# A two-layer diffusion-transformer block with attention, convolution and expert lookup: shorter lead of queries and routing, and a re-spaced plan of hosted work

## What is computed

```python
y, y_x = token_mixer(modulate(x, sh1, sc1), modulate(ctx, xsh1, xsc1), w_in, ...)   # dense GQA, short conv, banded attention, gates, w_out
x = layer_norm(alpha * x + g1 * y, ln1_g, ln1_b)
f = peer(modulate(x, sh2, sc2), w_pq, sub_keys, u_tab, v_tab)
x = layer_norm(alpha * x + g2 * f, ln2_g, ln2_b)
# (the same for ctx in layer 0)

def peer(...):                                  # one block of 128 tokens
    q = (xb @ w_pq).reshape(128, 8, 2, 128)     # 8 heads, two halves
    s = einsum('thpd,hpnd->thpn', q, sub_keys)  # 128 keys each half
    s1, i1 = top_k(s[:, :, 0], 16); s2, i2 = top_k(s[:, :, 1], 16)
    cand = s1[..., :, None] + s2[..., None, :]  # 256 pairs
    top, pos = top_k(cand, 16); expert = i1 * 128 + i2 at pos
    g = softmax(top)
    u = u_tab[expert]; v = v_tab[expert]        # 16384 experts a layer
    return einsum('thk,thkd->td', gelu(einsum('td,thkd->thk', xb, u)) * g, v)
```

## Time and profile before

| what | us |
|---|---|
| median of 3 runs | 4705.17 |
| lowest, highest | 4694.17, 4723.45 |
| the profiled execution | 4714.67 |
| its span (first to last instruction) | 4712.6 |
| TensorE, VectorE, ScalarE, GpSimd busy | 3173.5, 2879.9, 830.9, 2790.2 |
| moved by DMA | 1718.66 MB, mean 365 GB/s |

### The profile page before, as it was taken

One profiled execution on the slowest core, in us unless ns is written; L12 is line 12 of the kernel. 1 busy time (PEld: TensorE's weight loads), 2 busy tenths in 40 slices (PEclk: granted clock), 3 DMA queues, 4 the chain that ended last, 5 costly groups with the idle time before them and its releaser, 6 DMA issues.

```text
span 4712.6 us, 47030 instructions
## 1 busy us (share of the span) xinstructions
PE 3173.5 (67%) x16180; PEld 1609.4 (34%) x16180; DVE 2879.9 (61%) x7309; ACT 830.9 (18%) x1946; POOL 2790.2 (59%) x2623
## 2 busy tenths in 40 slices
PE   7977787977778887655653786767797845433333
PEld 4443354444444344322320432544444422200000
DVE  4865566466676587456766652476646766665652
ACT  1321213122122131101110110210312211010000
POOL 1125565457666676666677664046655677777776
PEclk8988897998888988767765898888898976666656
DMA  8879999999999999999999998489999999999998
GB/s 314 321 274 402 371 407 350 369 365 383 401 395 379 409 363 400 407 402 392 392 345 354 410 398 339 145 308 405 335 377 375 380 388 389 366 366 353 371 361 327
DMA packets 494093, 1718.66 MB, mean 365 GB/s; under 512 B 54177, under 2 KB 74913, under 8 KB 493473
## 3 DMA queue, kind: packets, MB, share of 16 engines
q0 software_dynamic: 375552, 1367.51, 75.6%
q1 hardware_dynamic: 100640, 335.04, 18.5%
q10 hardware_dynamic: 17664, 13.11, 0.8%
HBM read 1700.25 MB, written 15.20 MB: 364 GB/s over the span
## 4 chain that ended last, share of the span: by engine, by line
PE 32%; POOL 23%; DMA 15%; issue 12%; DVE 10%; another core or an unknown queue 5%; ACT 3%; SPq 0%; ACTq 0%; POOLq 0%; DVEq 0%
PE ps L967 30%; POOL vr L940 12%; POOL ur L927 10%; DMA vr<-in_v_tab,idxT 10%; DVE ur L2023 2%; PE ps L970 2%; DMA ur<-in_u_tab,idx 2%; DMA wring<-in_w_gb 1%; ACT arena L1429 1%; DVE mx L1891 1%; DMA wring<-in_w_mod 1%; POOL ur L940 0%; DMA wring<-in_w_qkv 0%; DMA wring<-in_w_out 0%
## 5 line engine op out<-in xcount | busy, mean ns | idle before, releaser
L2023 DVE CUSTOM_DVE_ANT_0 ur<-ur,hn 128x1024 f32<-128x1024 f32 x1280 | 1561.7, 1220 | 812.1 <-DMA ur<-in_u_tab,idx 732.6
L940 POOL DMA_INDIRECT vr<-in_v_tab,idxT x1256 | 1381.0, 1100 | 930.9 <-PE ps L967 499.0
L927 POOL DMA_INDIRECT ur<-in_u_tab,idx x1280 | 1357.3, 1060 | 787.1 <-issue 364.5
L967 PE MATMUL ps<-vr,spread 128*32 128x512 f32 x5024 | 896.7, 827 | 927.1 <-DMA vr<-in_v_tab,idxT 842.1
L967 PE MATMUL ps<-wring,arena 128*128 128x512 f32 x2240 | 1033.5, 612 | 76.8 <-ACT arena L1429 23.8
L967 PEld LDWEIGHTS ps<-vr,spread 128*32 128x32 f32 x5024 | 182.5, 135 | 1436.8 <-issue 1426.1
L967 PEld LDWEIGHTS ps<-wring,arena 128*128 128x128 f32 x2240 | 421.3, 195 | 628.3 <-issue 554.9
L967 PE MATMUL ps<-hT,wring 128*128 128x128 f32 (+1 forms) x2048 | 332.7, 321 | 30.5 <-DMA wring<-in_w_pq 22.8
L967 PEld LDWEIGHTS ps<-hT,wring 128*128 128x128 f32 x2048 | 300.7, 207 | 104.4 <-issue 62.6
L967 PE MATMUL ps<-arena,wring 128*128 128x258 f32 (+1 forms) x960 | 225.2, 394 | 7.3 <-issue 5.8
L970 PE MATMUL ps<-ident,arena 128*128 128x128 f32 x888 | 154.2, 311 | 110.7 <-issue 39.5
(11 more groups left out here) (204 smaller groups left out, 2941.9 us busy)
## 6 DMA issues: line engine op xcount, KB each, us to landing
wring<-in_w_gb SPq DMA_DIRECT2D x224, 512.0 KB
wring<-in_w_pq SPq DMA_DIRECT2D x128, 512.0 KB
wring<-in_w_qkv SPq DMA_DIRECT2D x68, 512.0 KB
wring<-in_w_out SPq DMA_DIRECT2D x64, 512.0 KB
wring<-in_w_conv SPq DMA_DIRECT2D x60, 512.0 KB
wring<-in_w_mod SPq DMA_DIRECT2D x48, 512.0 KB
vr<-in_w_modt POOLq DMA_DIRECT2D x48, 512.0 KB
ur<-in_u_tab,idx POOLq DMA_INDIRECT x1280
```

The lines of the kernel that those rows point to most:

```text
L927: nc.gpsimd.indirect_dma_start(u, None, u_rows, bass.IndirectOffsetOnAxis(ap=idx[:, at:at + 1], axis=0)).then_inc(landed, 16)
L940: nc.gpsimd.indirect_dma_start(v, None, v_rows, bass.IndirectOffsetOnAxis(ap=idxT[:, pair % 3, i:i + 1], axis=0)).then_inc(landed, 16)
L967: return nc.tensor.matmul(o, lhsT, rhs, start=first, stop=last, skip_group_check=True)
L2023: v.tensor_tensor_reduce(u, u, hn[:], 1.0, 0.0, ALU.mult, ALU.add, dots[:, j % 2, k:k + 1]).then_inc(s["dots_done"], 1)
```

## The change

`LEAD` is 2 and `LAG` is 1. `lead(n)` makes the queries and scores of two heads and the routing of one. A head's routing runs in the first eight slots of the head before it, two steps in each; ScalarE's exponential moves from slot 11 to slot 5. TensorE's transposition of the picks moves from slot 1 to slot 10, and `turn_picks` on VectorE from slot 3 to slot 10, of the same head. The `turn` steps move to slots 93 to 98, and the blocks of hosted work are re-spaced around them; the attention of tile 3 stays in tile 1, its `merge_last` moves to slots 0 to 16 of tile 2. A second modulation frees the banks, and `merge_far` has a wait for the copy of hn, because of the new order.

```diff
-LEAD = 3
-LAG = 2
+LEAD = 2
+LAG = 1
...
-        for jj, st in ((0, 0), (0, 1), (0, 2), (1, 0), (0, 3), (1, 1), (1, 2), (0, 4), (2, 0), (1, 3), (2, 1), (2, 2), (1, 4)):
+        for jj, st in ((0, 0), (0, 1), (0, 2), (1, 0), (0, 3), (1, 1), (1, 2), (0, 4)):
...
             put(near_part(1, team=1) + merge_first(1) + ending(1), 0, 62)
-            put(keys_job(1), 62, 74)
-            put([[("turn", 1)], [("row", 0)], [("row", 1)], [("row", 2)]], 74, 78)
-            put(keys_job(2) + queries_job(1) + conv_job(1), 78, 126)
+            put(keys_job(1) + keys_job(2), 62, 82)
+            put(queries_job(1), 82, 96)
+            put([[("turn", 1)], [("row", 0)], [("row", 1)], [("row", 2)]], 96, 100)
+            put(conv_job(1), 100, 126)
         elif n == 1:
-            put(near_part(2, 3, team=2) + merge_first(2) + ending(2), 0, 84)
-            put([[("turn", 2)]], 84, 85)
-            put(ending(3), 86, 126)
+            put(near_part(2, 3, team=2) + merge_first(2) + ending(2), 0, 96)
+            put([[("turn", 2)]], 97, 98)
+            put(attention([(3, q) for q in range(4, 8)]), 99, 126)
         elif n == 2:
-            put(queries_job(2)[0:1], 0, 1)
-            put(queries_job(2)[1:] + conv_job(2), 3, 34)
-            put([loads_of(4, 5, team=3)], 34, 35)
-            put(near_part(4, 5)[1:], 36, 74)
-            put([[("turn", 3)], [("row", 3)]], 74, 76)
-            put(merge_first(3), 78, 126)
+            put(merge_last(3), 0, 16)
+            put(queries_job(2)[0:1], 16, 17)
+            put(queries_job(2)[1:] + conv_job(2), 19, 46)
+            put([loads_of(4, 5, team=3)], 46, 47)
+            put(near_part(4, 5)[1:], 48, 78)
+            put(merge_first(3)[0:16], 78, 94)
+            put([[("turn", 3)], [("row", 3)]], 95, 97)
+            put(merge_first(3)[16:], 98, 126)
         elif n == 3:
             put(ending(4, 5), 0, 66)
             put(keys_job(3), 66, 82)
-            put([[("turn", 4)], [("turn", 5)]], 82, 85)
-            put(modulations(BY_PRODUCT[4:]), 84, 126)
+            put(modulations(BY_PRODUCT[4:6]), 83, 92)
+            put([[("turn", 4)], [("turn", 5)]], 93, 96)
+            put(modulations(BY_PRODUCT[6:]), 98, 126)
...
         elif n == 6:
             put(ending(7), 0, 30)
             put(queries_job(4)[0:1], 30, 31)
-            put(queries_job(4)[1:] + conv_job(4), 34, 70)
-            put([loads_of(8, 9, team=5)], 70, 71)
-            put([[("turn", 7)], [("row", 4)], [("row", 5)], [("row", 6)]], 74, 78)
-            put(near_part(8, 9)[1:] + merge_first(5)[0:16], 78, 126)
+            put(queries_job(4)[1:] + conv_job(4), 33, 62)
+            put([loads_of(8, 9, team=5)], 62, 63)
+            put(near_part(8, 9)[1:], 64, 94)
+            put([[("turn", 7)], [("row", 4)], [("row", 5)], [("row", 6)]], 95, 99)
+            put(merge_first(5)[0:16], 100, 126)
         elif n == 7:
-            put(merge_first(5)[16:], 0, 28)
-            put(ending(8, 9), 28, 82)
-            put([[("turn", 8)], [("turn", 9)]], 82, 85)
+            put(merge_first(5)[16:], 0, 26)
+            put(ending(8, 9), 26, 92)
+            put([[("turn", 8)], [("turn", 9)]], 94, 97)
...
-                    if b == MODS + 4:
+                    if b in (MODS + 4, MODS + 6):
                         free_banks(("mod", b, st))
...
                 if part == 0:
+                    w.wait_ge("hn_done", BEFORE["ga", m, hf, 0]["hn"])
                     w.wait_ge("pts_done", DONE["ev", ended_with(m)[-1], 7])
...
-                if k == 1 and j % 2 == 0 and j < end:
+                if k == 10 and j % 2 == 0 and j < end:
                     w.wait_ge("idx_done", j + 2)
-                    w.wait_ge("spread_done", j // 2 - 1)
+                    w.wait_ge("spread_done", j // 2)
                     w.wait_ge("it_done", j // 2)
                     w.wait_ge("sc_copied", min(j + LEAD, end))
                     by_picks(2 * P, idxf[:, j // 2 % 2, :], "it_mm")
...
-                if i + LAG < heads and k == 11:
+                if i + LAG < heads and k == 5:
                     exp_top(j + LAG)
...
-                if k == 3 and j % 2 == 0:
-                    if 2 <= i <= heads:
-                        w.wait_ge("ct_mm", j // 2)
-                    if i < heads:
-                        turn_picks(j // 2)
-                    if 2 <= i <= heads:
-                        spread_pair(j // 2 - 1)
-                if i + LAG < heads:
-                    route_step(j + LAG, k)
+                if k == 3 and j % 2 == 0 and 2 <= i <= heads:
+                    spread_pair(j // 2 - 1)
+                if k == 10 and j % 2 == 0 and i < heads:
+                    turn_picks(j // 2)
+                if i + LAG < heads and k < TOPK // 2:
+                    route_step(j + LAG, 2 * k)
+                    route_step(j + LAG, 2 * k + 1)
```

More of the change, by code:

```diff
@@ L1324, in peer @@
                     four_sums(P * FIRST[l] + row - 3)
-                if k == 1 and j % 2 == 0 and j < end:
-                    w.wait_ge("idx_done", j + 2)
-                    w.wait_ge("spread_done", j // 2 - 1)
-                    w.wait_ge("it_done", j // 2)
-                    w.wait_ge("sc_copied", min(j + LEAD, end))
-                    by_picks(2 * P, idxf[:, j // 2 % 2, :], "it_mm")
                 if k == 2 and j % 2 == 0 and i >= 2 and j <= end:
@@ L1344, in peer @@
                         key_scores(j + LEAD)
+                if k == 10 and j % 2 == 0 and j < end:
+                    w.wait_ge("idx_done", j + 2)
+                    w.wait_ge("spread_done", j // 2)
+                    w.wait_ge("it_done", j // 2)
+                    w.wait_ge("sc_copied", min(j + LEAD, end))
+                    by_picks(2 * P, idxf[:, j // 2 % 2, :], "it_mm")
             for at, steps in PLAN:
```

## The result

The changed kernel takes 4762.1 us (median of 5 runs, 4755.5 to 4788.9) against 4705.2 (median of 5 runs too), so the medians stand 57 us apart. The kernel is slower by about 1%, where I forecast faster by 11 us, and lies above my range. The profiled execution is the slowest of its five and spans 4786.9 us against 4712.6: of these 74 us, 17 come from which execution was profiled.

A forecast was written before the change was run, and what follows sets the result against it. By stretch, DMA engines (with gathers in bare tiles) or TensorE set the time, so edits only fill holes. Won 56, lost 45: net -11 us, 4694 us from the median, 0.2% faster; range 4625 to 4750.

The forecast's parts named there:

- Two steps a slot: Routing packed into a head's first eight slots: 0 in bare tiles, nearer waits in hosted ones; 6 us lost, ends 0 and 50.
- rival A: Hosted tiles: VectorE's wait for the picks at slot 10 takes over, +49 us, 4743 us; chance 0.17.
- where it is below nothing: Any stretch where TensorE's need minus the DMA's need is below nothing: bound by DMA, so its density costs nothing.
- The lead: Before each layer's first dot, VectorE routes one head, not two: 6 to 9 us won per layer, 15 for both.
- Tile 6's late chunk: Tile 6, query chunk queued behind loads of tiles 8 and 9: moving those loads ends TensorE's 18.9 us wait, 12 us won.
- The two reloads: SyncE's reloads of xT, closer behind a merge in tile 2 and a slot earlier in tile 6: 7 and 2 us lost.
- Tile 2: Takes over tile 3's last merge, so its other work is squeezed: its windows were to lengthen by 20 to 30 us.
- Tiles 6 and 7: Merge chunks spread over more slots, thinner attention, late query chunk gone: the two tiles were to lose 25 us.
- B: GpSimd's waits on TensorE fall well beyond the stretched parts, by a tenth, 72 us: 4635 us; chance 0.25.
- C: TensorE's clock falls in the stretched merge of tile 1, costing 33 us more: 4727 us; chance 0.08.
- D: The whole kernel: the change does not reach what bounds, the DMA engines hide all of it: 4705 us; chance 0.15.
- Bare tiles change: Sign of error: bare tiles 8 and 9, hosting nothing, were to stay at 2.8 to 2.9 us a slot.

The follow-up runs named there:

- Bursts alone: The kernel before, with two routing steps a slot in a head's first eight slots and the exponential at slot 5: 1.0096.
- picks: The kernel before, with only the picks' transposition and `turn_picks` moved to slot 10: 1.0017.
- both: The kernel before, with two routing steps a slot in slots 0 to 7, exponential at 5, and pick transposition and turn at 10; old lead and plan: 1.014.
- four steps: The kernel before, with four routing steps a slot in a head's slots 0 to 3, exponential in slot 11 and gates in slot 15: 1.0207.
- with room: The changed kernel, with queries and convolution of tiles 2 and 6 begun six slots later, so qkv chunks have time to land: 1.0092 to before.
- late gates: The changed kernel, with the exponential in slot 11 and the gate instructions in slot 15: 1.011 to before.
- bursts in bare tiles alone: The kernel before, with two routing steps a slot in the first eight slots and exponential at 5 only in tiles 4, 8 and 9: 1.0056.
- a denser packing of tiles 8 and 9: The kernel before, with four routing steps a slot in slots 0 to 3 in tiles 8 and 9 only; exponential at 11, gates at 15: 1.0005.
- taking about 70 us of gather time out of these two tiles: The kernel before, with the dots of tiles 8 and 9, slots 0 to 119, reading tokens from PSUM instead of the SBUF copy: 0.9981.
- bursts in all tiles: The kernel before, with two routing steps a slot in slots 0 to 7, exponential at 11 and gates at 15: 1.0125.
- The second half's price: The kernel before, with two routing steps a slot in a head's last eight slots and the exponential in slot 13: 1.0044.

## Why the prediction was wrong

**The step that failed** is "Two steps a slot". I summed VectorE's work, found 2.7 us a slot below 2.87, put bare tiles at 0 and took 6 for the whole. Bursts alone measured 45 us, picks 8, both 66. That the bursts are the greater part is shown by their own run. Why they cost that much is shown only in part. The sum of busy time left out that an instruction of VectorE can hold one of GpSimd: GpSimd was busy 52 us longer with the bursts, and where its queue is full that is time. Rows 6 could not warn me: their gathers of 0.94 us run beside VectorE's routing, or begin after the dot. In the main loop the mean over all GpSimd instructions was 1.06 (2790.2 by 2623), a number to ask about. The end of 50 that I named had the size, but a wrong cause (rival A), so that it comes near is luck.

**The bounds.** I wrote "where it is below nothing, a stretch is bound by DMA and its density is free", and of a bare slot of 2.87 us that "the gathers and the DMA engines set it". Both leave out a second bound that I did not price: two gather instructions and their issue, 2.58 us in the faster group and 2.84 with four steps. With four steps it binds there.

**The remaining sum** was won 56, lost 39 without the coupling, net 17. The changed kernel (1.0097) against both parts in the old plan (1.014, another chip) has 20 us, and with room on one chip 23. The net came near partly by luck, for its terms did not. The lead: the first dot of layer 0 came at 294.9 us before and 287.6 after, but it scatters from 288.7 to 296.4 over all traces with the long lead and from 284.0 to 287.6 with the short one, so 5 us on average; from the last dot of layer 0 to the first of layer 1 it is 181.0 and 177.2, on average 180.6 and 174.8. That is about 11 of my 15. Tile 1 gave 20, with the attention. Tile 6's late chunk, 12, was worth 0 by its own run, though its window fell by 10.5 us: a window's gain came back elsewhere. The two reloads, 9 lost, made longer waits than I said and cost nothing. Tile 2 lost 39 where I said 20 to 30, with bursts in it; in two other pairs of traces it lost 23 (late gates) and 11 (with room, against picks alone). Tiles 6 and 7 gained nothing together (858.5 to 867.7), the merge's 10 in slots 32 to 64 of tile 7 given back by 18 in the next window, where the attention of tiles 8 and 9 now stands.

**The rivals.** A: the wait is there (93.5 us alone, 123.8 in the changed kernel) and its price is 0.17%, 8 us; most of such a wait lies in a stretch that others bound. B falls: GpSimd's waits on TensorE went 499 to 480 and on the dots up by 36. C falls: the granted clock in tile 1's window is 1.00, as before. D falls: the time moved by 1%, and parts of the change reach the bound in both directions. "Bare tiles change" was my own sign of being wrong; they changed by 12 us of 735 in one execution, which is not clear of scatter, and the run with bursts in bare tiles alone (1.0056) shows it better.

**What stays open.** How the 45 us of the bursts split between held gathers and VectorE late for other work. On the two faster groups (4582, 4584) bare tiles alone gave 1.0056 of 1.0096. On the slower chips the held gathers of bare tiles are not it: a denser packing of tiles 8 and 9 cost nothing (4721), and taking about 70 us of gather time out of these two tiles changed the time by -9 us, within noise (4753), while bursts in all tiles cost 1.0125 (4716). The profiled chip, with a bare slot of 2.87 us, is nearer to these. So on it most of the 45 us should lie in tiles 0 to 7, whether by held gathers there or by late dots and hosted steps; no run separates the two. The second half's price (1.0044), with no longer gathers at all, says that part of the cost is something else again.

## What to carry to other kernels

When small work is packed beside a stream of gathers, sum each engine's time, and then ask whether its instructions lengthen those of its neighbour: compare the mean duration of the gather in the main loop with its least, and line up the end of the long ones with the end of what ran beside them. Price every queue that feeds the bound, with its issue gaps; the one just under the bound can take over on a faster chip. Then ask whether the stretch is bound by it at all, before you call the longer instructions the cost. Do not bank a stall because it has a large number: three such waits (18.9 us for a query chunk and 50 for two qkv chunks removed, one of 457 for the exponential added) left the time where it was.

## What the runs showed of the hardware

An indirect gather of 128 rows occupies GpSimd for 0.94 us, with 0.30 us to the next. If an fp32 dot of VectorE with both inputs in SBUF is under way as it starts, it ends 0.8 us after the dot, up to 1.99 us in all (796 of the 863 gathers over 1 us in the kernel before). With one input of the dot in PSUM all 133 gathers of a window of tile 8 took 0.93 to 0.95 us. A dot that began 0.33 us after the gather did not hold it. Small dependent instructions of VectorE placed back to back made it busy 54 us longer over the kernel (2884.2 to 2938.6), for the same count; one other instruction between them takes most of that away (2898.8). The same program differs by 4% between chips (4582 to 4753 us) and by 0.8% on one chip at two times (4716, 4753), and a bare slot took 2.58 us on one and 2.87 on another.
